# Softmax denominators of an attention stage, formed from ones and the weights of all four key blocks on TensorE

## The reference, cut to what matters

```python
s = einsum('bkgqd,bskd->bkgqs', q, k) * scale      # 512 queries x 512 keys, a head
p = softmax(s, axis=-1)
o = einsum('bkgqs,bskd->bkgqd', p, v)              # 64 values a head
```

## Time and profile before

| | us |
|---|---|
| median of 3 runs | 1500.31 (1497.65 to 1500.95) |
| the profiled execution | 1497.4 |
| its span, first to last instruction | 1495.4 |
| TensorE busy | 1385.5 (93%) |
| VectorE busy | 919.3 (61%) |
| ScalarE busy | 569.5 (38%) |
| POOL busy | 547.8 (37%) |

### The profile page before, as it was taken

How to read it: one execution, slowest core, us unless ns; L and a number is a source line. 1 busy time by engine, 2 the same in 40 slices (tenths; PEclk the granted TensorE clock), 3 DMA queues, 4 the chain that set the end, 5 groups by cost and what they waited for, 6 DMA issues and landing times. The chain is left out here.

```text
span 1495.4 us, 14534 instructions
## 1 busy us (share of the span) xinstructions
PE 1385.5 (93%) x5599; PEld 1006.5 (67%) x5599; DVE 919.3 (61%) x945; ACT 569.5 (38%) x803; POOL 547.8 (37%) x263
## 2 busy tenths in 40 slices
PE   5999988887999999999979997988979999999997
PEld 3677643355788888778746784433748888887885
DVE  4766876556678878721176778654467887874212
ACT  4422344443543443422242325344344434433322
POOL 2312331015444444444452215210354444444444
PEclk8999999998999999999989999999989999999997
DMA  7212310012233333233241223000213333332331
GB/s 243 87 29 64 78 30 15 0 39 74 71 99 90 94 99 94 86 89 99 83 141 45 69 53 76 15 0 0 84 51 90 99 91 93 99 97 79 102 92 67
DMA packets 205469, 112.46 MB, mean 75 GB/s; under 512 B 15239, under 2 KB 202361, under 8 KB 204506
## 3 DMA queue, kind: packets, MB, share of 16 engines
q1 hardware_dynamic: 205402, 111.54, 25.8%
HBM read 105.63 MB, written 2.10 MB: 72 GB/s over the span
## 5 line engine op out<-in xcount | busy, mean ns | idle before, releaser
L473 POOL TENSOR_TENSOR wl<-raw,wh 128x1024 fp32r<-128x1024 f32 x184 | 445.9, 2425 | 761.1 <-ACT wh L547 761.1
L547 ACT ACTIVATE wh<-raw 128x1024 fp32r<-128x1024 f32 x184 | 194.9, 1059 | 593.4 <-PE ps L957 553.9
L955 PE MATMUL ps<-gh,wh 128*128 128x512 f32 (+1 forms) x896 | 362.7, 405 | 7.5 <-POOL wl L473 7.5
L956 PE MATMUL ps<-gl,wh 128*128 128x512 f32 (+1 forms) x896 | 354.1, 395 | 0.0
L957 PE MATMUL ps<-gh,wl 128*128 128x512 f32 (+1 forms) x896 | 354.0, 395 | 0.0
L955 PEld LDWEIGHTS ps<-gh,wh 128*128 128x128 f32 (+1 forms) x896 | 167.9, 187 | 52.9 <-issue 13.6
L956 PEld LDWEIGHTS ps<-gl,wh 128*128 128x128 f32 (+1 forms) x896 | 167.9, 187 | 43.8 <-issue 4.1
L957 PEld LDWEIGHTS ps<-gh,wl 128*128 128x128 f32 (+1 forms) x896 | 167.9, 187 | 41.1
L1777 DVE SCALAR_TENSOR_TENSOR cv<-pad,pm,cv 128x512 f32<-128x512 f32 x88 | 130.4, 1482 | 83.3 <-ACT cv L857 83.3
L1367 DVE TENSOR_TENSOR acc<-acc,sq 128x512 f32<-128x512 f32 x24 | 60.7, 2531 | 192.4 <-ACT sq L591 192.2
L955 PE MATMUL ps<-fh,wh 128*128 128x512 f32 x352 | 139.1, 395 | 3.3 <-POOL wl L473 3.3
(11 more groups left out here) (243 smaller groups left out, 1910.6 us busy)
## 6 DMA issues: line engine op xcount, KB each, us to landing
raw<-w_up SPq DMA_DIRECT2D x88, 512.0 KB, 3.8
raw<-w_down SPq DMA_DIRECT2D x32, 512.0 KB, 4.0
raw<-w_in SPq DMA_DIRECT2D x30, 512.0 KB, 4.0
raw<-w_out SPq DMA_DIRECT2D x16, 512.0 KB, 4.1
raw<-w_down SPq DMA_DIRECT2D x16, 384.0 KB, 3.4
xio<-x SPq DMA_DIRECT2D x4, 512.0 KB, 4.5
win<-c_win SPq DMA_DIRECT2D x2, 1024.0 KB, 4.9
TF<-c_tf SPq DMA_DIRECT2D x2, 1024.0 KB, 9.5
```

The source lines that it names most:

```text
L473: nc.gpsimd.tensor_tensor(wl[:, slot, :], raw[:, slot, :], wh[:, slot, :].bitcast(F32), ALU.subtract).then_inc(S["lo_ready"], 1)
L547: A(wh[:, slot, :], raw[:, slot, :], ACT.Copy).then_inc(S["hi_ready"], 1)
L955: mm(ps[0:cols, bank, :], w_hi, x_hi, start=start and k == 0, stop=False)
L956: mm(ps[0:cols, bank, :], w_hi, x_lo, start=False, stop=False)
```

## The change

The sums over halves of the keys, their buffer (its place is kept by one of the same size) and their semaphore go. denominators takes all four blocks of keys of each head from probT: eight f32 matmuls instead of four. exp, which overwrites a buffer of probT in heads from 4 on, waits for den_mm of the pair that last used it, where it waited for summed.

```diff
-        tsum = sb("tsum", [P, 2, 2, T])
+        spare = sb("spare", [P, 4, T])
...
                         act.wait_ge(S["pv"], lay * PAIRS + (h - 4) // 2 + 1)
-                        act.wait_ge(S["summed"], lay * HEADS + h - 3)
+                        act.wait_ge(S["den_mm"], lay * PAIRS + (h - 4) // 2 + 1)
                     A(probT[h % 4][:, sc, :], ps[:, S_BANK(h, sc), :], ACT.Exp).then_inc(S["p_ready"], 1)
...
                 def denominators(p):
 
                     free7("den", p)
-                    pe.wait_ge(S["summed"], lay * HEADS + 2 * p + 2)
-                    for part in range(2):
+                    pe.wait_ge(S["p_ready"], lay * N_TILES + (2 * p + 2) * TC)
+                    for sc in range(TC):
                         for half in range(2):
-                            ins = mm(ps[half * GD:(half + 1) * GD, 7, :], ones[:, 0:GD], tsum[:, half, part, :],
-                                     start=(part == 0), stop=(part == 1))
+                            ins = mm(ps[half * GD:(half + 1) * GD, 7, :], ones[:, 0:GD], probT[(2 * p + half) % 4][:, sc, :],
+                                     start=(sc == 0), stop=(sc == TC - 1))
                     ins.then_inc(S["den_mm"], 1)
...
-                def row_sums(h):
-
-                    dve.wait_ge(S["p_ready"], lay * N_TILES + (h + 1) * TC)
-                    if h >= 2:
-
-                        dve.wait_ge(S["den_mm"], lay * PAIRS + h // 2)
-                    pT = probT[h % 4]
-                    tt(tsum[:, h % 2, :, :], pT[:, 0:2, :], pT[:, 2:4, :], ALU.add).then_inc(S["summed"], 1)
...
                     if h >= 4 and h % 2 == 0:
                         pair_out((h - 4) // 2)
-                    if h:
-                        row_sums(h - 1)
...
                         pair_out(PAIRS - 2)
-                        row_sums(HEADS - 1)
                         group_norm(1)
```

More of the change, by code:

```diff
@@ L249, in build @@
                 "ha_mm", "hu_copy", "he_mm", "ho_mm", "he_copy", "h_prod", "hc_mm", "h_done",
-                "q2hi", "q2lo", "m_hi", "n_tile", "nmax", "shift", "s_tile", "p_ready", "summed", "pv", "den_mm", "den_inv",
+                "q2hi", "q2lo", "m_hi", "n_tile", "nmax", "shift", "s_tile", "p_ready", "pv", "den_mm", "den_inv",
                 "y_pair", "q_roped",
```

## The result

The changed kernel takes 1510.58 us (median of 4 runs, 1509.32 to 1512.71), the kernel before 1500.63 (4 runs, 1497.65 to 1502.30): a ratio of 1.0074, 95% interval 1.0054 to 1.0095, about 10 us slower. The profiled execution took 1509.32 us, span 1507.4, 12.0 more than the span before.

A forecast was written before the change was run, and what follows sets the result against it. TensorE was taken to bound attention, VectorE behind it. A layer: 6.84 us for pairs 0 to 3, minus 2.25 early, plus 0.85 at the end, 5.4; both layers, 10.7 slower, on the median 1511.0 us, range 1504 to 1519.

The forecast's parts named there:

- 1.71 us for each added call's work: TensorE, denominators: four more steps of 0.43 us make each of 12 calls 1.71 us longer, 10.3 us a layer.
- The alternatives, 0.28 or 1.2 us a step: Bounds for a denominators step: 0.28 at the projections' pace (13.5 us more), 1.2 if halves run in turn (57 us).
- the rule on weight loads: Denominators: loads overlap only across different row groups, so added loads are paid in full, 13 us on top, 1524; chance 0.02.
- What comes back early: 2.25 us a layer: Early heads of attention: TensorE idling for VectorE that goes with the sums, 2.25 us a layer taken back.
- Head 2: TensorE's wait for maxima before peaks of head 4: without the sum of head 1, 1.0 us comes back.
- head 4: TensorE's wait for maxima before peaks of head 5: without the late sum of head 2, 1.1 us comes back.
- q_lo: A POOL operation slowed once a layer beside the sum of head 0: 0.15 us comes back.
- The pauses that stay: TensorE's pauses of 1.31 us at group(0) and 1.35 us before peaks of heads 9 and 11 keep their length.
- The end of a layer: 0.85 us of 3.42: Last two denominators calls: 3.42 us added, pauses for yl and acc at the output projection vanish, 0.85 us remains.
- exp's new wait, the same size of spare: nothing: ScalarE's exp waiting for den_mm is already met, and the equal-sized spare moves no address: no cost.
- The sum: Both layers together: 5.4 us a layer, 10.9 for two, stated as 10.7 us slower.
- the clock: TensorE's slow first 22 us of attention might vanish, 1.8 us a layer, 1507.5; chance 0.03, an equal loss elsewhere as likely.

The follow-up runs named there:

- x1_matmuls_alone: Kernel before with TensorE taking all four key blocks for the denominators while VectorE keeps its now unread sums; 1520.2 us, ratio 1.0142.
- x6_twice: Changed kernel with each matmul of the denominators issued twice; 1551.5 us, ratio 1.0343 to the kernel before.
- x3_last_pairs: Kernel before with the change applied only to pairs 4 and 5, the last two denominators calls of a layer; 1501.7 us, ratio 1.0013.
- x5_one_part: x4_sums_moved with VectorE also adding the two parts of each head's sum, so 2 denominators matmuls a pair instead of 4; 1493.7 us, ratio 0.9955.
- x11_one_part_late: x4_sums_moved plus 9 unread TensorE matmuls a layer in pauses, with sums reduced to one part from head 4 on; 1485.0 us, ratio 0.9889.
- x2_sums_gone: Changed kernel with denominators taking key blocks 0 and 1 only, so as many matmuls as before and no sums; 1496.6 us, ratio 0.9982.
- x4_sums_moved: Kernel before with all VectorE sums kept but moved in its order, using four sum buffers instead of two; 1497.9 us, ratio 0.9991.

## Why the prediction was right

The median came out at 1510.6 us, forecast 1511.0. Step by step:

- *1.71 us for each added call's work.* Right: 3.59 - 1.86 = 1.73 in the trace, 6.9 us for four calls in x1_matmuls_alone, and the same price for twice as many in x6_twice. The alternatives, 0.28 or 1.2 us a step, are out. So is the rule on weight loads as the prediction read it: 16 records with 16 loads of 0.136 us take 3.59 us, less than 8 steps of 0.43 and the loads together.
- *What comes back early: 2.25 us a layer.* Too small: 17.02 to 15.77 us ahead of call 0, and 6.86 to 5.45 from call 0 to call 4, 2.7 in all. Head 2 gave 1.0 as forecast; head 4 gave 1.25 instead of 1.1; q_lo 0.3 instead of 0.15; and a wait of 0.2 us for a lo part in head 4, which I had left among the small losses that were not listed.
- *The pauses that stay.* Right: 1.31 and 1.35 us, unchanged.
- *The end of a layer: 0.85 us of 3.42.* Right in kind, 0.64 in the trace, alone in x3_last_pairs 0.63. The traces also show where the 0.2 us between went. Call 5 starts 6.92 us after call 4, where 5.32 + 1.71 would be 7.03: that is the wait for the sum of head 11, for which I had allowed 0.1 but which I had left out of the total. From call 5 to the projection 0.04 less was added than forecast, and the two pauses hid 2.63 us instead of 2.57.
- *exp's new wait, the same size of spare: nothing.* Right; exp waits for scores alone.
- *The sum.* 4.8 us a layer, 9.6 in all, where I forecast 10.7: both errors are on the same side. Two low stretches of 1.4 us, in head 7 of layer 0 and at the third tile of layer 1's output projection, brought the profiled execution back to 12.0 us over. In the medians the two nearly met: 10.0.

What the prediction undervalued was the clock. It looked at the stretch that is slow in the kernel before, and gave a chance of 0.03 to its vanishing and as much to a new one elsewhere. New ones came, between executions of the same program as well as in the profiled execution of the change, and in the runs of the kernel before the clock goes with some 6 us of time. That the forecast of the time holds to 0.4 us is partly chance; that of the steps does not depend on it.

## What to carry to other kernels

The cost of moving work between two engines isn't the difference of the two pieces. TensorE's added 10.3 us a layer cost 4.8 because two pauses at the end of a stage took most of one part, and because VectorE's instruction had held up others that stood behind it in order. But that second benefit didn't need the move: putting the same VectorE work at other places of its program gave 3.4 us a layer with two more buffers, and kept TensorE's work low. In the time that was 6 to 7 us of 1500 with the clock held, and about 2 without. Ask of an instruction that waits what stands behind it, before asking which engine should do it.

## What the runs showed of the hardware

The granted clock fell in every trace at the three pauses of 6.6 us outside attention, and behind pauses of 1.3 to 2.6 us not each time: a pause of 3.09 us in x5_one_part (layer 1, before a tile of the input projection) and one of 3.74 in x11_one_part_late were followed by no fall, and one of 1.34 in the same x11_one_part_late was. Executions of the same program differ in it: the kernel before had mean clocks of 0.970 to 0.977 and 1496.3 to 1504.2 us. A gain can be lost in part to low stretches behind pauses that the kernel before has as well (x2_sums_gone: 7.6 us by the steps, 3 in the time). 9 unread matmuls a layer, in front of waits that were there anyway, raised the mean clock. In the kernel before it went from 0.971-0.977 to 0.977-0.980, and the time fell by 6.8 us; in x4_sums_moved it went from 0.968-0.972 to 0.978-0.979, and the time fell by 10.5. What decides whether the clock falls behind a given pause stays open.
